# Hybrid GLA, attention and RG-LRU backbone on one core: later key-value products and tile sums, decay logits in split products, split gate products in both layers

## The reference

```python
# gated linear attention (GLA), 4 heads, DK 128, DV 256, chunks of 64, both directions d
log_a[d] = log_sigmoid(lr[d] @ w_dec[d] + b_dec[d]) / 16        # lr: 16 columns of h @ w_in
cum = cumsum(log_a); q_dec = q * exp(cum); k_inv = k * exp(-cum); k_end = k * exp(total - cum)
o = tril(q_dec @ k_inv.T) @ v + q_dec @ s
s = exp(total) * s + k_end.T @ v                                 # state, chunk by chunk

# attention, 8 query heads and 2 key/value heads of 128
q, k = rope(rms_norm(q)), rope(rms_norm(k));  out = softmax(q @ k.T / sqrt(128)) @ v

# RG-LRU, 8 blocks of 128 channels, both directions d
z = einsum('bnhi,ghij->gbnhj', x, w_gates[d]) + b_gates[d]       # two gates
log_a = -8 * sigmoid(z[0]) * softplus(-lam); u = sqrt(1 - exp(2 * log_a)) * sigmoid(z[1]) * x
h = scan(exp(log_a) * h + u)
```

## Time and profile before

| | |
|---|---|
| median of 3 runs | 1884.93 us (1883.0 to 1885.36) |
| the profiled execution's own time | 1882.9 us |
| its span in the trace | 1881.1 us |
| TensorE busy | 1832.6 us (97%) |
| VectorE busy | 1356.2 us (72%) |
| ScalarE busy | 990.5 us (53%) |
| mean granted TensorE clock | 0.998 |

### The profile page before, as it was taken

One profiled execution on the slowest core, in us unless ns is written; L12 is line 12 of the kernel. 1 busy time (PEld: TensorE's weight loads), 2 busy tenths in 40 slices (PEclk: granted clock), 3 DMA queues, 4 the chain that ended last, 5 costly groups with the idle time before them and its releaser, 6 DMA issues.

```text
span 1881.1 us, 25703 instructions
## 1 busy us (share of the span) xinstructions
PE 1832.6 (97%) x10280; PEld 1530.1 (81%) x10280; DVE 1356.2 (72%) x1981; ACT 990.5 (53%) x1420; POOL 39.4 (2%) x86
## 2 busy tenths in 40 slices
PE   7999999999999999899999998999999999989998
PEld 4778778888888888578888886888778888989997
DVE  5666547635788888889888787765656788578874
ACT  5543445546766324653444335633536898466663
POOL 1000010000000000000000000000100000000000
PEclk9999999999999999999999999999999999999999
DMA  9212222223344555235544553222323454545564
GB/s 351 69 57 63 79 73 63 86 82 101 98 138 135 190 191 190 78 113 168 169 167 143 197 208 131 69 67 74 112 73 101 152 163 153 184 140 167 181 183 130
DMA packets 68854, 248.72 MB, mean 132 GB/s; under 512 B 8304, under 2 KB 8320, under 8 KB 68608
## 3 DMA queue, kind: packets, MB, share of 16 engines
q1 hardware_dynamic: 64800, 234.91, 38.1%
q0 software_dynamic: 3360, 10.08, 1.8%
q10 hardware_dynamic: 576, 2.10, 0.3%
HBM read 243.39 MB, written 1.05 MB: 130 GB/s over the span
## 4 chain that ended last, share of the span: by engine, by line
PE 80%; DVE 14%; ACT 3%; issue 2%; POOL 0%; DVEq 0%; ACTq 0%; POOLq 0%
PE ps L1662 57%; PE ps L1645 4%; DVE wlo L937 4%; PE ps L1654 3%; DVE fa L987 2%; PE ps L1692 2%; PE ps L1980 2%; ACT whi L488 1%; PE ps L2055 1%; DVE state L1332 1%; PE ps L1889 1%; PE ps L1867 1%; PE ps L1971 1%; DVE xc L987 1%; PE ps L1943 1%
## 5 line engine op out<-in xcount | busy, mean ns | idle before, releaser
L937 DVE TENSOR_TENSOR wlo<-wraw,whi 128x1024 fp32r<-128x1024 f32 x350 | 426.0, 1221 | 217.5 <-ACT whi L488 216.8
L488 ACT ACTIVATE whi<-wraw 128x1024 fp32r<-128x1024 f32 x350 | 368.1, 1054 | 221.8 <-PE ps L1662 195.8
L1662 PE MATMUL ps<-hh,whi 128*128 128x512 f32 (+1 forms) x1632 | 367.2, 347 | 3.5 <-DVE fa L987 2.3
L1662 PE MATMUL ps<-hl,whi 128*128 128x512 f32 (+1 forms) x1632 | 363.2, 345 | 0.0
L1662 PE MATMUL ps<-hh,wlo 128*128 128x512 f32 (+1 forms) x1632 | 334.5, 346 | 0.0
L1662 PEld LDWEIGHTS ps<-hh,whi 128*128 128x128 f32 x1632 | 268.9, 190 | 45.1 <-issue 6.8
L1662 PEld LDWEIGHTS ps<-hl,whi 128*128 128x128 f32 x1632 | 270.2, 190 | 37.4 <-issue 1.6
L1662 PEld LDWEIGHTS ps<-hh,wlo 128*128 128x128 f32 x1632 | 262.6, 190 | 38.9 <-issue 4.4
L965 DVE SCALAR_TENSOR_TENSOR ps<-wada,cond 128x1024 f32<-128x1024 f32 x144 | 173.3, 1244 | 0.0
L987 DVE SCALAR_TENSOR_TENSOR fa<-ps,par,fa 128x510 f32<-128x510 f32 (+1 forms) x176 | 100.0, 610 | 9.8 <-ACT fa L590 8.0
L1662 PE MATMUL ps<-bh,whi 128*128 128x512 f32 (+1 forms) x384 | 85.3, 344 | 0.0
(11 more groups left out here) (339 smaller groups left out, 2745.3 us busy)
## 6 DMA issues: line engine op xcount, KB each, us to landing
wraw<-in_weights SPq DMA_DIRECT2D x350, 512.0 KB, 3.5
wada<-in_w_ada_rows SPq DMA_DIRECT2D x80, 512.0 KB, 3.6
ada_first<-in_w_ada SPq DMA_DIRECT2D x14, 512.0 KB, 15.6
wgate<-in_w_gate POOLq DMA_DIRECT2D x16, 256.0 KB, 2.9
q_turned<-aq POOLq DMA_DIRECT2D x32, 64.0 KB, 2.3
x<-in_xt ACTq DMA_DIRECT2D x2, 512.0 KB, 7.5
x<-in_xt SPq DMA_DIRECT2D x2, 512.0 KB, 7.3
ada_first<-in_w_ada ACTq DMA_DIRECT2D x2, 512.0 KB, 12.1
```

The source lines that it names most:

```text
L488: A_(whi[u % HI][:], wraw[RING_W[u] % RAW][:], ACT.Copy).then_inc(s_hi, 1)
L937: V.tensor_tensor(wlo[s][:], wraw[s][:], whi[u % HI][:].bitcast(F32), ALU.subtract).then_inc(s_lo, 1)
L1662: ins = mm(dst[:, r, c:], w[:, kk, r * P:(r + 1) * P], x_[:, UK * h + kk, c:], start=h == 0 and k in (0, 2) and kk == 0, stop=h == m - 1 a ...
```

## The change

- `SPLIT_GATES` becomes (0, 1): the second layer's gate products are split too, with `gate_his` on ScalarE and `gate_los` on VectorE for each of its eight blocks.
- The decay weights and `lr` are split (`wdec_hi`, `lr_hi` by ScalarE; `wdec_lo`, `lr_lo` by VectorE), and `decays(h)` is six fp32r matmuls in place of two plain float32 products.
- `decays(0)` stands behind the first two parts of the unit that followed it.
- `gla_kv(h, 2)` and `gla_kv(h, 3)` stand one part later.
- `tile_stat` of the loop over heads stands two parts later, in both layers.

The diff, without the declarations of buffers and semaphores:

```diff
-SPLIT_GATES = (0,)
+SPLIT_GATES = (0, 1)
...
                 make_h(l, 2 * l, nt0, 0)
+                act.wait_ge(s_wdec, 16 * (l + 1))
+                A_(wdec_hi[:], wdec[:], ACT.Copy).then_inc(s_wdh, 1)
                 softplus()
...
-                A_(lr[:], ps[:, 7, :], ACT.Copy).then_inc(s_lr, 1)
+                A_(lr_hi[:], ps[:, 7, :], ACT.Copy).then_inc(s_lr, 1)
...
+                dve.wait_ge(s_wdh, l + 1)
+                V.tensor_tensor(wdec_lo[:], wdec[:], wdec_hi[:].bitcast(F32), ALU.subtract).then_inc(s_wdl, 1)
                 edge(u0 + 2)
+                dve.wait_ge(s_lr, l + 1)
+                V.tensor_tensor(lr_lo[:], ps[:, 7, :], lr_hi[:].bitcast(F32), ALU.subtract).then_inc(s_lrl, 1)
                 softplus()
                 edge(u0 + 3)
-                dve.wait_ge(s_lrp, l + 1)
...
-                        ins = mm(ps[:, 4 + d], wdec[:, d, h * DK:(h + 1) * DK], lr[:], start=True, stop=True)
+                        cols = slice(h * DK, (h + 1) * DK)
+                        mm(ps[:, 4 + d], wdec_hi[:, d, cols], lr_hi[:], start=True, stop=False)
+                        mm(ps[:, 4 + d], wdec_hi[:, d, cols], lr_lo[:], start=False, stop=False)
+                        ins = mm(ps[:, 4 + d], wdec_lo[:, d, cols], lr_hi[:], start=False, stop=True)
...
                 first_pairs(u0, 2 * l)
-                pe.wait_ge(s_lr, l + 1)
-                pe.wait_ge(s_wdec, 16 * (l + 1))
+                parts(u0 + 4, 0, 2)
+                pe.wait_ge(s_wdl, l + 1)
+                pe.wait_ge(s_lrl, l + 1)
                 decays(0)
-                parts(u0 + 4, 0, 12)
+                parts(u0 + 4, 2, 12)
...
                     gla_kv(h, 1)
-                    parts(u, 10, 13)
+                    parts(u, 10, 14)
                     gla_kv(h, 2)
-                    parts(u, 13, 18)
+                    parts(u, 14, 19)
                     gla_kv(h, 3)
-                    parts(u, 18, 20)
+                    parts(u, 19, 20)
                     gla_out(h)
...
                         att_out(k)
+                        parts(ub, b + 3, b + 5)
                         if h + 2 < AQ:
                             tile_stat(AKV + h + 2, 7)
-                        parts(ub, b + 3, b + 7)
+                        parts(ub, b + 5, b + 7)
...
                         att_out(h)
+                        parts(ub, b + 5, b + 7)
                         if h + 2 < AQ:
                             tile_stat(AKV + h + 2, 7)
-                        parts(ub, b + 5, min(b + 11, 15 * AQ))
-                        parts(ub, min(b + 11, 15 * AQ), min(b + 15, 15 * AQ))
+                        parts(ub, b + 7, min(b + 15, 15 * AQ))
```

More of the change, by code:

```diff
@@ L193, in build @@
         cs, scanmask = at("cs", C, [P, 2, SEQ]), at("scanmask", C + 1, [P, NCH, CHUNK])
-        wdec = at("wdec", C + 2, [P, 2, HEADS * DK])
+        wdec, wdec_lo = (at(n, C + 2, [P, 2, HEADS * DK], dt) for n, dt in (("wdec", F32), ("wdec_lo", F32R)))
+        wdec_hi = at("wdec_hi", C + 4, [P, 2, HEADS * DK], F32R)
         cond = at("cond", C, [P, 2, AK, AC])
@@ L216, in build @@
         go = at("go", M + 47, [P, TOK // P, DV])
-        lr = at("lr", M + 49, [P, TOK])
+        lr_hi, lr_lo = (at(n, s_, [P, TOK], F32R) for n, s_ in (("lr_hi", M + 49), ("lr_lo", C + 6)))
         atts = tiles("atts", M + 50, 1)
@@ L303, in build @@
         s_ahi, s_alo = sem("att_hi"), sem("att_lo")
+        s_wdh, s_wdl, s_lrl = sem("decay_weights_hi_made"), sem("decay_weights_lo_made"), sem("lr_lo_made")
         s_ghi, s_glo = sem("gate_his_made"), sem("gate_los_made")
```

## The result

The changed kernel takes 1891.45 us (median of 5 runs, 1889.96 to 1898.42), the kernel before took 1884.93 in the same rounds (1882.78 to 1887.06). The ratio is 1.0042, 95% interval 1.0031 to 1.0052: slower, by 6.5 us of the medians. The profiled execution is the one of 1891.45 us, its span is 1889.7.

What follows compares the result with a forecast made beforehand. TensorE, 97% busy, was taken as the bound, with a 14.32 us ScalarE-VectorE loop close under it in the second layer's recurrence. Terms 5.4 - 2.1 + 3.1 - 3.1 - 1.3 + 3.8 = +5.8 on 1884.9 gave 1890.7 us; range 1879 to 1895.5.

Steps and rivals of the forecast that it cites:

- gate products split, second layer: Second layer's recurrence: ScalarE's two copies a block lengthen a loop that TensorE must follow; +5.4 us, bounds -5.7 and +10.
- decay logits, heads 1 to 3: GLA, both layers: split products save 0.35 us a head on TensorE; -2.1 us (to -3.1).
- `decays(0)` later, less its own split: Before each layer's first `gla_att`: no slack, so 1.57 us filled ahead returns as a stall in both layers; +3.1 us.
- key-value products: GLA, both layers: one part more covers eight waits of TensorE for `state`; -3.1 us, or 0 to -3.1.
- tile sums, first layer: First layer's attention: eight matmuls, 1.92 us, cover a wait of 1.30 us; -1.3 us.
- tile sums, second layer: Second layer's attention, heads 2 and 3: sums 1.92 us later feed chains already late; +3.8 us, lower bound 0.
- Loop, period and place: Second layer's recurrence, table load to table load: copies inside the loop, 14.32 + 1.04 = 15.36 us, over TensorE's 14.24.
- the round "counted as slack": Second layer's recurrence: one of seven loop rounds left out, so the last table load gets six times 1.04 us.
- The rival of busy time alone: Second layer's recurrence: only busy time counts, stage from 119.4 to 116.7 us, -2.7, kernel 1882.6 us; chance 0.10.
- The 0 at heads 0 and 5: Second layer's attention: TensorE's wait for the sum itself only moves to the `scores` on the same tile; 0 us.
- The waits before `gla_att`: Sign in the profile: TensorE idle some 1.6 to 2 us before the first `gla_att` of each layer.
- The one at `scores` for head 4: Sign in the second layer's attention: TensorE's wait there grows from 0.70 to about 2.6 us.

Runs made afterwards that it cites:

- 4: The kernel before with one edit, the second layer's gate products split: 1890.50 us, ratio 1.0036.
- 7: As 5, with `gla_kv(h, 2)` and `gla_kv(h, 3)` back at their old places: 1879.82 us, ratio 0.9971.
- 2: The changed kernel with `decays(0)` ahead of the unit's parts again, still split: 1887.04 us, ratio 1.0016.
- 3: The changed kernel with the second layer's tile sums right behind `att_out` again: 1888.02 us, ratio 1.0011.
- 10: As 5, with the second layer's tile sums two parts later at heads 2 and 3 alone: 1883.09 us, ratio 0.9992.
- 9: As 5, but second-layer gates split, ScalarE's copies ahead of the tanh for `l_ti`, VectorE's remainders behind `lru_in`, both a block earlier: 1877.54 us, ratio 0.9966.
- 5: The changed kernel with plain second-layer gate products, `decays(0)` ahead of the unit's parts, second-layer tile sums right behind `att_out`: 1876.52 us, ratio 0.9952.
- 1: The changed kernel with plain float32 gate products in the second layer again: 1888.18 us, ratio 1.0018.

## Why the prediction was right

The forecast was 1890.7 us, and 1891.45 came. The terms, each against the stage that holds it:

| term | predicted us | measured us |
|---|---|---|
| gate products split, second layer | +5.4 | +5.5 (6.3 alone, with a half clock, 4) |
| decay logits, heads 1 to 3 | -2.1 | -2.1 (six of eight in 7) |
| `decays(0)` later, less its own split | +3.1 | +4.8 (3.6 + 1.9 in 2, less 0.7) |
| key-value products | -3.1 | -3.7 (7) |
| tile sums, first layer | -1.3 | -1.6 |
| tile sums, second layer | +3.8 | +5.2 (3), 3.7 at two heads (10) |
| sum | +5.8 | +8.1 |

- **Gate products.** Loop, period and place held: 15.36 us predicted, 15.37 measured. I had the last of seven rounds at 94.5 us behind the first (88.77 + 6.24 - 0.5), and it came 94.46 behind (1482.26 to 1576.72). Between seven loads lie six rounds, and the sum prices all six, so the round "counted as slack" isn't in it. The rival of busy time alone is out (4), but so is the idea that came with my theory, that only the copies' place costs: off the loop, they make TensorE's rounds shorter and still win nothing, since TensorE then waits 1.59 and 1.97 us in two other places, the second for ScalarE to take the last block (9). ScalarE is busy 115.0 us of the 119.5 from 1455.8 to 1575.3 there, and TensorE 115.7; whether ScalarE's work in all or the order of the last blocks sets the end is not shown.
- **`decays(0)`.** The chain had no slack, as read; the step that was mis-sized is the price of a stall. I gave it its own length, and in the first layer TensorE's clock halved behind it, some 1.7 us more. The same for the tile sums: the wait of 3.01 us had some 1.4 us of half clock behind it. These 3.1 us, less the 0.9 that the key-value products and the first layer's sums gave beyond their forecast, are why the measured sum is 2.3 us over the predicted one.
- **Tile sums, second layer.** Heads 2 and 3 carry it, 3.7 of the 3.9 us without the half clock. The 0 at heads 0 and 5 holds: their waits of 1.08 and 1.47 us are 1.06 at `scores`, and 0.52 and 0.74 in two places, after.
- **What the profile was to show.** The waits before `gla_att` were forecast at 1.6 to 2 us and are 1.84 and 2.12; those at the gate products at 1.1 and are 0.88 in most blocks; the one for `xc` at 3.1 and is 3.01. The one at `scores` for head 4 was forecast at 2.6 and is 1.59: 0.29 us of the delay is taken up by another wait for `xc` ahead of it, and another 0.35 were never there: in 3 and 5, with the sums in their old place, this wait is 0.35 and not 0.70, and VectorE no longer stands 0.46 us before `aq` as it did in the earlier trace rows. No run says why, nor where the last 0.4 us went; by the stage's end the two heads have lost 3.7 us all the same.
- **Key-value products and the first layer's sums** gave a little more than their waits.
- **Sum and medians.** The stages that the edits touch give 7.9 us in the profile, the rows that no edit touches 0.8 more, the medians 6.5, the ratio 7.9 (0.0042 x 1884.9). The near hit to 0.8 us is partly luck: the terms are good to some 2 us in all.

The rule of occupancy (the Trainium skill, "Perfetto Trace Analysis", Identifying the Most-Contended Engine), read without the reservation that it makes for TensorE, pointed to TensorE, 97% busy. The trace disagrees for this edit: TensorE's busy time fell by 4.0 us and the time rose by 6.5. The Trainium skill also says ("Perfetto Trace Analysis", Optimization Strategy) that the most-contended engine can change over time within a kernel. By busy time no row here shows that: in the second layer's recurrence TensorE was busy all of the 119.4 us and ScalarE 108.4. What bound that stage after the edit was a loop over ScalarE and VectorE, which neither engine's busy share shows.

## What to carry to other kernels

In this kernel, work taken off the busiest engine paid only where the helper work that it needs stood outside the loops and chains that are just as long; so close the loop over the other engines (from one table load to the next) and compare it with the busiest engine's period, before splitting anything. When something is moved later to cover a wait, follow who waits for its result: here the key-value products and the first layer's sums had nobody behind them and paid in full, while head 0's decay logits in both layers and the second layer's sums at heads 2 and 3 fed chains without slack and lost nearly every microsecond that they were moved. Undoing the three edits that lose and keeping the three that pay gives 1876.5 us, 0.9952 of the kernel before.

## What the runs showed that I had not expected

A stall of TensorE can cost more than its length. Behind the waits of 1.84 us (74.23) and 3.01 us (1406.94) the granted clock is 0.62 and 0.59 in the windows above, and the work behind the first took 7.37 us from `gla_att` to the next decay logits (74.23 to 81.60) where it took 5.72 before (73.24 to 78.96). It doesn't follow from the length of the wait alone: the second layer's wait of 2.12 us at `gla_att` had no half clock behind it, and the wait of 3.01 us for `xc` had one in the changed kernel and in 1, and none in 2 and 10; the wait of 2.54 us in the second layer's recurrence had one in 2, 3 and 4 and none in the changed kernel. Such stretches also stand at the boundaries between stages, in the kernel before too (granted clock 0.50 at 1158.9 and 1176.0 us), and come and go from one profile to the next. They go with what the table shows in rows that no edit touches: the row of the first layer's recurrence and FFN stands at 1.3 to 1.6 us in the eight profiles that have one near 795 us, and at -0.1 to 0.1 in the four that have none there (7, with two near it, has 2.2). So one profile beside another is good to 1 or 2 us for the whole kernel, and to 0.1 for a stage only where neither has such a stretch in it.
